# Splitting 66 tiles of the expert table during the projection, and fetching them with transposing DMAs

## The reference, cut to what matters

```python
xn = rms_norm(h, g_mix[l]); proj = xn @ w_in[l]
...
s = jnp.einsum('thpd,hpkd->thpk', q, sub_keys)
s_top, i_top = lax.top_k(s, PEER_TOPK)
...
h = jnp.einsum('td,ted->te', xc, jnp.take(u, ic, axis=0))
a = jax.nn.gelu(h, approximate=False) * gc
return jnp.einsum('te,ted->td', a, jnp.take(v, ic, axis=0))
```

## Time and profile before

| what | value |
|---|---|
| median of 3 runs | 3213.93 us (3206.36 to 3214.76) |
| the profiled execution | 3208.9 us |
| its span, first to last instruction | 3207.2 us |
| mean granted clock of TensorE | 0.953 |
| busy: PE, DVE, ACT, POOL | 95%, 72%, 31%, 40% |
| moved by DMA | 594.91 MB, mean 185 GB/s |
| project_in | 0 to about 305 us |
| retrieve | about 704 to 1079 us |
| spread_weights | about 1079 to 1610 us |
| experts | from about 1611 us |

### The profile page before, as it was taken

One profiled execution on the slowest core, in us unless ns is written; L12 is line 12 of the kernel. 1 busy time (PEld: TensorE's weight loads), 2 busy tenths in 40 slices (PEclk: granted clock), 3 DMA queues, 4 the chain that ended last, 5 costly groups with the idle time before them and its releaser, 6 DMA issues. The chain is left out here.

```text
span 3207.2 us, 49336 instructions
## 1 busy us (share of the span) xinstructions
PE 3043.3 (95%) x17450; PEld 1711.2 (53%) x17450; DVE 2321.1 (72%) x4680; ACT 1004.6 (31%) x1471; POOL 1279.3 (40%) x899
## 2 busy tenths in 40 slices
PE   8898889889999699999969999999999999999999
PEld 4444645445555477777635555555555554444444
DVE  3234465438999666666558888888888888999996
ACT  4322255323343355555411222222222222222221
POOL 1021111002443212212156666666655555555662
PEclk9999567899999799999989999999999999999999
DMA  3210010121121244555488888878888888888884
GB/s 106 70 40 0 14 40 1 34 79 55 64 73 52 93 175 186 196 196 185 171 283 287 271 292 280 274 272 289 287 275 274 272 273 287 303 305 292 309 293 174
DMA packets 256174, 594.91 MB, mean 185 GB/s; under 512 B 20768, under 2 KB 127408, under 8 KB 252976
## 3 DMA queue, kind: packets, MB, share of 16 engines
q1 hardware_dynamic: 180016, 318.63, 29.3%
q0 software_dynamic: 73728, 268.47, 23.7%
q10 hardware_dynamic: 2304, 6.29, 0.6%
HBM read 513.63 MB, written 79.69 MB: 185 GB/s over the span
## 5 line engine op out<-in xcount | busy, mean ns | idle before, releaser
L238 PE MATMUL f_y<-f_v_hi,f_a_hi 128*128 128x512 f16 x1536 | 583.5, 380 | 9.5 <-DVE p_h L2212 9.5
L239 PE MATMUL f_y<-f_v_lo,f_a_hi 128*128 128x512 f16 x1536 | 583.3, 380 | 0.0
L240 PE MATMUL f_y<-f_v_hi,f_a_lo 128*128 128x512 f16 x1536 | 583.3, 380 | 0.0
L2179 POOL DMA_INDIRECT f_rows<-in_peer_u,p_row_index x256 | 355.9, 1390 | 207.0 <-DVE f_rows L2220 124.4
L2179 POOL DMA_INDIRECT f_rows<-in_peer_v,p_row_index x256 | 310.9, 1215 | 280.7 <-DVE p_h L2230 252.4
L2220 DVE SCALAR_TENSOR_TENSOR f_rows<-f_rows,p_xs 128x1024 f32<-128x1024 f32 x256 | 379.8, 1517 | 46.5 <-DMA f_rows<-in_peer_u,p_row_index 46.5
L2230 DVE SCALAR_TENSOR_TENSOR p_h<-f_rows,f_row_a,p_h 128x1024 f32<-128x1024 f32 x256 | 394.3, 1540 | 17.6 <-DMA f_rows<-in_peer_v,p_row_index 10.8
L2212 DVE SCALAR_TENSOR_TENSOR p_h<-f_y,p_h 128x512 f32<-128x512 f32 x384 | 262.9, 685 | 109.5 <-PE f_y L240 107.5
L2190 POOL TENSOR_TENSOR f_v_lo<-f_v_in,f_v_hi 128x1024 f16<-128x1024 f32 x128 | 283.6, 2216 | 145.0 <-ACT f_v_hi L2154 143.7
L238 PE MATMUL f_hid<-p_act_hi,x_u_hi 128*128 128x384 f16 x1008 | 330.5, 328 | 2.0 <-DVEq L2197 2.0
L239 PE MATMUL f_hid<-p_act_lo,x_u_hi 128*128 128x384 f16 x1008 | 330.3, 328 | 0.0
(11 more groups left out here) (311 smaller groups left out, 5461.4 us busy)
## 6 DMA issues: line engine op xcount, KB each, us to landing
f_v_in<-in_peer_v SPq DMA_DIRECT2D x128, 512.0 KB, 5.2
dense_weights<-e_stage SPq DMA_DIRECT2D x24, 2048.0 KB, 8.7
f_g_in<-dense_weights SPq DMA_DIRECT2D x32, 1536.0 KB, 15.6
x_u_in<-in_peer_u SPq DMA_DIRECT2D x64, 512.0 KB, 4.9
e_u_in<-in_peer_u SPq DMA_DIRECT2D x48, 512.0 KB, 4.1
x_gel<-early_tiles SPq DMA_DIRECT2D x64, 384.0 KB, 3.4
early_tiles<-e_gel SPq DMA_DIRECT2D x48, 384.0 KB, 2.5
a_w_in<-in_w_in SPq DMA_DIRECT2D x24, 512.0 KB, 3.8
```

The lines of the kernel that those rows point to most:

```text
L238: pe.matmul(out, a_hi, b_hi, start=first, stop=False)
L239: pe.matmul(out, a_hi, b_lo, start=False, stop=False)
L240: return pe.matmul(out, a_lo, b_hi, start=False, stop=last)
L2179: nc.gpsimd.indirect_dma_start(out=rows[q % ROWS][:], out_offset=None, in_=table, in_offset=bass.IndirectOffsetOnAxis(ap=T.row_index[:, ti ...
```

## The change

In project_in, a `Splitter` loads tiles of u as they lie in HBM (rows on partitions), writes both halves beside them and stores the pair in HBM as `u_split`. Tiles 0 to 47 go through ScalarE (high) and VectorE (low), in a ring of four buffers in T.dv and T.dk; 12 of them stand in column qk, 4 in ga, 16 in gv, 8 in gr, 8 in dq. Tiles 48 to 65 go through GpSimd alone (three instructions each), in a ring of two in T.dq, ahead of GpSimd's work for dq. SP moves both sorts: after every second tile of the first sort comes one of the second. Retrieve and spread fetch a pair with one DMA that transposes, straight into the operand's buffer; `turn`, `split` and `low` are gone, and with them their waits. A fetch now waits until both hidden halves of the buffer's last tile are done. experts is as it was. SP's loops in retrieve and spread, and the inner loops of the later columns on ScalarE and VectorE, are written out.

```diff
+class Splitter:
...
+    def load(self, sp, i):
+        if i >= self.ring:
+            sp.wait_ge(self.lo_done, i - self.ring + 1)
+        sp.dma_start(self.u_in[i % self.ring], self.u_rows[self.first + i]).then_inc(self.loaded[i % self.ring], 16)
+
+    def store(self, sp, i):
+        sp.wait_ge(self.lo_done, i + 1)
+        sp.dma_start(self.T.u_split[self.first + i], self.halves[i % self.ring].rearrange("p x d -> p (x d)")).then_inc(
+            self.stored[i % self.ring], 16)
+
+    def transfers(self, sp, i):
+        self.store(sp, i)
+        if i + self.ring < self.count:
+            self.load(sp, i + self.ring)
+
+    def ready(self, eng, i):
+        eng.wait_ge(self.loaded[i % self.ring], 16 * (i // self.ring + 1))
+        if i >= self.ring:
+            eng.wait_ge(self.stored[i % self.ring], 16 * (i // self.ring))
+
+    def high(self, act, i):
+        self.ready(act, i)
+        b = i % self.ring
+        self.nc.scalar.activation(self.halves[b][:, 0], self.u_in[b], ACT.Copy, scale=S_U).then_inc(self.hi_done, 1)
+
+    def low(self, dve, i):
+        b = i % self.ring
+        dve.wait_ge(self.hi_done, i + 1)
+        self.nc.vector.scalar_tensor_tensor(self.halves[b][:, 1], self.u_in[b], S_U, self.halves[b][:, 0], ALU.mult,
+                                            ALU.subtract).then_inc(self.lo_done, 1)
+
+    def both(self, pool, i):
+        self.ready(pool, i)
...
+        self.nc.gpsimd.tensor_scalar(self.u_in[b], self.u_in[b], S_U, None, ALU.mult).then_inc(self.scaled, 1)
...
+        self.nc.gpsimd.tensor_copy(self.halves[b][:, 0], self.u_in[b]).then_inc(self.hi_done, 1)
...
+        self.nc.gpsimd.tensor_tensor(self.halves[b][:, 1], self.u_in[b], self.halves[b][:, 0],
+                                     ALU.subtract).then_inc(self.lo_done, 1)
...
+SPLITS = {"qk": 12, "ga": 4, "gv": 16, "gr": 8, "dq": 8}
+SPLIT_SV = sum(SPLITS.values())
+SPLIT_G = 18
...
+        U = Splitter(nc, io, T, S, "u", 0, SPLIT_SV, [T.dv, T.dk])
+        G = Splitter(nc, io, T, S, "g", SPLIT_SV, SPLIT_G, [T.dq])
...
-            for c in range(1, len(COLS)):
-                for q in range(PIECES):
-                    load_w(c, q)
+            for i in range(U.ring):
+                U.load(sp, i)
+            for i in range(G.ring):
+                G.load(sp, i)
+            for q in range(PIECES):
+                load_w(1, q)
+            for q in range(PIECES // 2):
+                load_w(2, q)
+            for c in range(len(COLS)):
+                if c:
+                    for q in range(PIECES // 2):
+                        if c + 1 < len(COLS):
+                            load_w(c + 1, q + PIECES // 2)
+                    for q in range(PIECES // 2):
+                        if c + 2 < len(COLS):
+                            load_w(c + 2, q)
+                for i in splits(COLS[c][0], 0, 1):
+                    U.transfers(sp, i)
+                    if i % 2 and i // 2 < SPLIT_G:
+                        G.transfers(sp, i // 2)
...
+            for i in range(SPLIT_G):
+                G.both(pool, i)
...
+                    for i in splits("qk", r):
+                        U.high(act, i)
...
+            for i in splits("ga", 0, 1):
+                U.high(act, i)
...
+                    for i in splits(name, t):
+                        U.high(act, i)
...
             const.tables(dve)
+            for i in splits("qk", 0, 1):
+                U.low(dve, i)
...
                     split_w(c)
+                if COLS[c - 1][0] not in gains:
+                    for i in splits(COLS[c - 1][0], 0, 1):
+                        U.low(dve, i)
                 if COLS[c - 1][0] == "gv":
...
+                (G if name == "dq" else U).all_stored(dve)
...
+                    for i in splits(name, t):
+                        U.low(dve, i)
...
-    def load(self, sp, c, b, again=True):
-        if again:
-            sp.wait_ge(self.u_turned, (c - 1) * self.ring + b + 1)
-        sp.dma_start(self.u_in[b][:], self.u_rows[c, b]).then_inc(self.u_loaded[b], 16)
+    def load(self, sp, c, b):
+        if c:
+            sp.wait_ge(self.hid_done, BASE + 2 * ((c - 1) * self.ring + b) + 2)
+        sp.dma_start(self.u[b][:].rearrange("p x k e -> p (x k) e"), self.u_rows[c, b],
+                     transpose=True).then_inc(self.u_loaded[b], 16)
...
         if half == 0:
-            pe.wait_ge(self.u_lo_done, BASE + n + 1)
+            pe.wait_ge(self.u_loaded[b], c * 16 + 16)
...
             for b in range(2):
-                rows = slice((N_EARLY + b) * P, (N_EARLY + b + 1) * P)
-                sp.dma_start(F.u_in[b][:], io.peer_u[0, rows, :]).then_inc(next_loaded, 16)
...
+                for x, half in enumerate((F.u_hi, F.u_lo)):
+                    sp.dma_start(half[b][:], T.u_split[N_EARLY + b, :, x * D:(x + 1) * D],
+                                 transpose=True).then_inc(next_loaded, 16)
```

More of the change, by code:

```diff
@@ L1419, in load_w @@
                 sp.dma_start(w_in[:], w_v[h]).then_inc(w_loaded, 16)
-            def step(hh, b, first=False, last=False):
-                h = 2 * hh + b
-                if not last:
+            sp.sem_inc(w_loaded, 16)
+            for r in range(EARLY_R):
+                E.load(sp, 0, r)
+            sp.wait_ge(w_lo_done, 1)
+            load_w(1)
+            for h in range(PEER_H):
+                if h + 2 < PEER_H:
                     sp.wait_ge(w_lo_done, h + 2)
                     load_w(h + 2)
-                if not (first and b == 0):
+                if h:
                     E.load(sp, h, 1)
-                if not (last and b):
+                if h + 1 < PEER_H:
                     E.load(sp, h + 1, 0)
-            sp.sem_inc(w_loaded, 16)
-            for r in range(EARLY_R):
-                E.load(sp, 0, r, again=False)
-            sp.wait_ge(w_lo_done, 1)
-            load_w(1)
-            for b in range(2):
-                step(0, b, first=True)
-            with sp.Fori(1, PAIRS - 1) as hh:
-                for b in range(2):
-                    step(hh, b)
-            for b in range(2):
-                step(PAIRS - 1, b, last=True)
             E.all_kept(sp, EARLY_R * PEER_H)
@@ L1476, in step @@
                 h = 2 * hh + b
-                before = not (first and b == 0)
-                if before:
-                    E.turn(pe, h - 1, 1)
-                else:
-                    E.turn(pe, h, 0)
                 if not (last and b):
@@ L1484, in step @@
                     scores(h + 1)
-                if before:
+                if not (first and b == 0):
                     E.hidden(pe, h - 1, 1, 0)
-                    E.turn(pe, h, 0)
                     E.hidden(pe, h - 1, 1, 1)
                 E.hidden(pe, h, 0, 0)
-                if last and b:
-                    E.turn(pe, h, 1)
                 E.hidden(pe, h, 0, 1)
@@ L1865, in _ @@
             step(NBLOCK - 1, True)
[L1867 to L1875 removed]
+            pe.wait_ge(next_loaded, 64)
             pe.wait_ge(E.gelu_done, BASE + 2 * EARLY_S * NBLOCK)
@@ L1901, in step @@
                         b, half = HALVES[s]
-                        if half == 0 and b + 1 < EARLY_S:
-                            E.split(act, blk, b + 1)
-                        elif half == 0 and not last:
-                            E.split(act, blk + 1, 0)
                         E.gelu(act, blk, b, half)
-            E.split(act, 0, 0)
             with act.Fori(0, NBLOCK - 1) as blk:
@@ L1918, in _ @@
                                      scale=1.0 / (S_U * S_ACT))
-        @block.gpsimd
-        def _(pool):
-            E.prime_gpsimd(pool)
-            with pool.Fori(0, NBLOCK) as blk:
-                for b in range(EARLY_S):
-                    E.low(pool, blk, b)
         @block.sync
```

160 lines of the change are left out of this document (57 added, 103 removed).

## The result

| | before | after |
|---|---|---|
| median of 4 runs each, us | 3211.31 (3206.36 to 3214.76) | 3236.62 (3231.22 to 3237.35) |
| span of the profiled execution | 3207.2 | 3235.3 |
| granted clock, mean | 0.953 | 0.940 |

The ratio is 1.0074 (95% interval 1.0057 to 1.0090): the change makes the kernel slower by about 25 us, where 13 were forecast. The direction and the range hold; the time lies 10 us above the forecast.

What follows compares the result with a forecast made beforehand. TensorE bounds spread, VectorE retrieval; with the change the DMA queues pace the projection. Projection +65 less spread 52, retrieval nothing, gives +13 us on the 3213.9 median: 3227, range 3190 to 3290 (likeliest case 3195 to 3275).

Steps and rivals of the forecast that it cites:

- Spread, forecast 51.5: Spread: 40.5 us saved in the body by removing TensorE's transposes, 6 at the start, 5 at the end; called 52.
- The fetches: Transposing DMA: 3 us a tile taken, between 1.36 and 4.5; 2.0 estimated from the Trainium skill; fits within spread's blocks.
- Rival (b): Spread: transposing DMA is slow, above 5.9 us a tile the queues bound it; at 8 us 3328; chance 0.12.
- Retrieval, forecast 0: Retrieval: 16 tiles lose transposes, copies and subtractions, worth nothing because VectorE's unbroken chain covers it; unchanged within 3 us.
- Projection, forecast +65: Projection: splitting 66 tiles delays gr's first result 58 us to 214.3, plus 5 in column dq and 2 for the clock.
- The piece: Projection: one load or store of 512 KiB, or weight piece, takes 1.30 us; 92 pieces until tile 31 take 120 us.
- dry time: Projection: 9 us in which queues run dry because SP waits for a subtraction, GpSimd or split weights; nothing to 25.
- from the bias to gr's first result: Projection: from VectorE adding the gate's bias to ScalarE's first result of gr, 28.0 us as in the kernel before.
- the queues therefore pace the projection: Projection: ScalarE's copies wait for loads and stores, and results freeing TensorE's accumulators stand behind them; 120 us of pieces.
- (a): Projection: queues don't pace it, loads and stores move side by side, gr's first result at 162; 3175 us; chance 0.22.
- (c): Projection: GpSimd paces SP, 10 us a tile instead of 5, +31 us over 14 pairs; 3258 us; chance 0.09.
- What to look for: Signs: gr's first result near 214, TensorE waits some 15 us before gv and 40 before gr, queue share 0.9 or more.

Runs made afterwards that it cites:

- experiment 1: Changed kernel with only six tiles split and every transposing fetch reading one of those six: 3155.28 us, ratio 0.9825 to the kernel before.
- experiment 2: Changed kernel with GpSimd working on 64 of 1024 columns from its third tile on, all transfers kept at full size: 3228.20 us in one run.
- experiment 6: Changed kernel with the gate's steps after dq's weights and gr's first two results, its scans after dq's weights: 3237.53 us, ratio 1.0077 to the kernel before.
- experiment 9: Experiment 6 with a ring of four weight pieces instead of two, loaded mid-column for the column after next: 3182.69 us, ratio 0.9916 to the kernel before.
- experiment 3: Changed kernel with GpSimd's work kept but only 64 columns loaded from its third tile on and 64 stored: 3216.48 us in one run.
- experiment 5: Changed kernel with eight of ScalarE's and VectorE's tiles moved from column gv to column gr: 3230.12 us in one run.

## Why the prediction was right, point by point

**Spread, forecast 51.5:** 54.8 (7.9 + 41.1 + 5.8). The body gave 41.1 for 40.5, the end 5.8 for 5, the start 7.9 for 6: the transposed tile was there after at most 5.9 us, as estimated, and TensorE's first wait there is for VectorE. The fetches are costed right as well: per block of 38.4 us the queues are busy for 0.65 x 38.4 = 25 us; less the 15.8 us of stores that is 2.3 us a tile, where 3 were taken. The estimate of 2.0 us from the Trainium skill (DMA: Bandwidth & Descriptors, section Latency and other measured facts) is the nearer one. The 261 GB/s of the Trainium skill behind it are for a non-contiguous middle dimension; whether that is this case, no run shows. Rival (b) falls: the median landing in spread is 4.8 us (view of e_u in experiment 1) and TensorE never waits for one in spread's body. Its block of 39.4 us should have been 38.3 by its own terms (41.8 less 3.5), which makes its threshold 5.6 us a tile; 38.4 was measured.

**Retrieval, forecast 0:** -3 to -4 (354.4 against 357.2, and 358.5 in two runs that undo it), at the edge of the 3 us that were allowed.

**Projection, forecast +65:** +79.2, and this is the term that was mis-sized. Step by step: the first tile was finished at 57.5 for 53.0, since the last tiles of x and ga's weights now share the queues with the first six tiles and VectorE's tables slip with them (+4.5). The piece, taken at 1.30 us, is 1.25 by experiment 2, but GpSimd's 7.0 us a tile (5 taken) and their coupling made of it 7.9 us a pair, so 1.31. Tile 31 landed at 191.9; after 57.5, 92 pieces of 1.31 and 2 us, 12 us of dry time are left where 9 were taken (+3.4 with the piece). Its copy and subtraction took 3.2 us for 2.3, and from the bias to gr's first result it took 32.7 us for 28.0. Those 4.7 us go with GpSimd's work: in experiment 2, where it hardly works, the same way takes 27.8, and VectorE's three steps on it (minimum, scans, first half of the weights) take 2.3, 4.5 and 2.8 us in place of 4.1, 6.0 and 4.5. Together 13.5: 227.9 for 214.3. Behind that, +7.8 for +7.

**The step that was wrong in kind** is the sentence that the queues therefore pace the projection, carried past tile 31. Up to tile 31 it holds: 0.91 of the queues on average, with the 12 us of dry time at the turns. Behind it the sum carries over 28.0 us from the bias to gr's first result as a fixed length. They weren't fixed: 9.6 of them had been a wait for weights before the change, and with all bytes and all work kept the ring and the gate's order bring gr's first result to 7.3 us behind tile 31. So the queues' rate sets 120 us of the sum, as forecast, but not the cost of 79: 45 us of that go by the ring alone (experiments 6 and 9), and of the 43.3 against the changed kernel 12 at most are there without splitting. The sum came near because it used the old length where the old wait was still present. That the total is only 15 us off between the spans (28.1 for 13) is partly luck too: +14 in the projection and +8 in the last stage met -3 in spread and -4 between.

On the rule of the Trainium skill that transfers between HBM and SBUF are bound at about 358 GB/s per core (DMA: Bandwidth & Descriptors, section Where 436 GB/s comes from): the windows of 25 us at 419 and 420 GB/s disagree, on this one core, and the piece of 1.46 us that it would give is not seen.

**Rivals.** (a), queues that don't pace, is out: a third of the tiles' bytes gone gave 18.5 us (experiment 3). (c), GpSimd paces, is half true: its tile takes 7.0 us, not 10, and its work is worth 11.6 us, its place in SP's order 2. What to look for named gr's first result near 214, waits of about 15 before gv and 40 before gr, and a queue share of 0.9 or more from 55 to 190: it was 227.9, 28.5 and 37.9, and a share of 0.90 on average but 0.62 at the first turn. The 28.5 us for 15 were the sign of the turns. The loss of 7.6 us in the last stage was in no step, and is mostly scatter.

What stays open: how the 45 us between experiments 6 and 9 divide between the ring's size and the earlier place of the loads, since no run changed one alone; what sorts the traces at the stage behind the projection; and why experiment 9 still waits 16.6 us before gv.

## What to carry to other kernels

Work that fills idle queues and engines inside another stage is paid for twice: by its own bytes and work (48 of 79 us here are left with the ring), and at that stage's turns (31 us), which the mean rate doesn't show. Count, for each transfer that the stage itself waits for, how long it now stands behind the new ones (here 4 weight pieces a column, 14 to 18 us of SP's time), and load those a whole turn ahead before adding the work. A chain carried over at its old length is worth asking about too, since something new may stand in it. And moving one late thing (experiments 5 and 6) shows little where the next thing in the same order is as late.

## What the runs showed of the hardware

- VectorE and GpSimd slow each other on float32 tiles in SBUF: VectorE's subtraction of 1024 columns takes 1.22 us with GpSimd nearly idle (experiment 2, all of them) and 1.5 to 1.6 beside it, its scan 2.28 against 3.03 us; GpSimd's multiplication takes 2.76 us with VectorE idle (at 99.17 us) and up to 3.74 beside it.
- A transposing DMA of 512 KB holds SP for about 2.2 us at its issue (four in 9.93 us), against 0.4 for a plain one. In spread this cost nothing, as SP has 38 us for four.
- Loads and stores side by side held 419 GB/s on this core, over 25 us in the changed kernel and over 45 in experiment 2 (145 to 190 us).
